# The down matrices of the expert loop issued from ScalarE's queue

## The chip, the cores and the metric

The kernel runs on one core of a Trainium2 chip. The metric is the device time of one launch in microseconds; lower is better. The core has five engines that run their own instruction streams: TensorE (PE), VectorE (DVE), ScalarE (ACT), GpSimd (POOL) and SyncE (SP). They meet through semaphores alone. SP and ACT can each start transfers (DMAs) on a queue of their own; sixteen DMA engines carry them out.

## What is computed

One layer of an encoder for 320 tokens (256 of one request group, 64 of another), all in float32: a mixing sublayer (a projection, attention beside a convolution, gates, an output projection, a layer norm) and then a sublayer of experts. The experts take most of the time:

```python
logits = (x @ w_router + b_router).astype(jnp.float32)
top_val, top_idx = lax.top_k(logits, TOP_K)            # 4 of 32
gate = jax.nn.softmax(top_val, axis=-1)
...
gt = jnp.minimum(xe @ w_gate[e] + b_gate[e], SWIGLU_LIMIT)
up = jnp.clip(xe @ w_up[e] + b_up[e], -SWIGLU_LIMIT, SWIGLU_LIMIT)
h = gt * jax.nn.sigmoid(SWIGLU_ALPHA * gt) * (up + 1.0)
return h @ w_down[e] + b_down[e]
```

Each expert has three matrices of 1024 x 1024 in float32. Each token goes through four experts, and the sum of their outputs, weighted with `gate`, goes into a second layer norm.

## The kernel before

The mixing sublayer and the router fill the first 430 us or so. What follows is the expert loop. The tokens of one expert are taken in groups of 32 slots, so an expert has one group or several, by how many tokens chose it. The router's counts are turned into tables in SBUF: `order` gives the expert at each of 32 places, `tbl[k]` the number of the first group of place k, `tbl[32]` the number of all groups. Experts 0 and 1 always stand at places 0 and 1, since their matrices are loaded ahead; behind them places 3, 6, 9, ... hold the experts with most tokens, in falling order, and the two places between them experts with few.

The weights have six buffers of 4 MB, two for each kind: `WG`, `WU` and `WD`, each with a buffer for even and one for odd places (`par`). Every matrix is loaded in two halves of 2 MB (`load_halves`, L237, which calls `load_half`, L234; the profile puts the DMA instructions of the loop under L235).

For one group PE does, in this order: the gate products (`gate_or_up`, matmuls L1334, biases L1339), the combine of the previous group's first token tile (L1349), the up products, the combine of the second tile, the gather of the next group's tokens (L1322), a small product (L1381), the combine of the third tile (L1351), and the down products (L1390). Gate and up wait for each half of their matrix (L1330), down likewise (L1388). PE raises `gate_half`, `gate_done`, `up_half`, `up_done`, `down_half` and `down_done`, once in each group.

VectorE clamps the gate (L948), waits for ScalarE's sigmoid, multiplies (L950), adds a tile of combined output to the accumulator (L938), does the same for up (L955, L958), transposes (L963), and so on. ScalarE has two steps in a group: the sigmoid (L614, with a table load ahead of it) and the copy of the down result out of PSUM (L616), after `down_done`. GpSimd makes the selection matrices (L454 to L463) and one-hot columns (L468, L469). VectorE, GpSimd and SP read the tables at every expert (`value_load`); ScalarE reads only the total number of groups, once (L610), and then runs one flat loop.

SP feeds the weights (L349 to L355). For each place from 2 on it reads `used`, the number of groups up to and including the place whose buffers are to be taken (two places earlier), and the expert's number `e`. Then it waits for `gate_half`, starts the first half of WG, waits for `gate_done`, starts the second half, and so on through WU and WD: twelve steps in strict order, all on SP's queue. Places 0 and 1 are loaded ahead of the loop. Behind it SP loads the rows of the last layer norm into WG[0] (L357 to L365).

Of the kernel before, what the change touches and what calls it, by code (L numbers as in the profile page):

```python
# [28 lines left out]
E = 32  # L29
# [16 lines left out]
def encoder_step(nc, x_prompt, x_sample, cache_k, cache_v, state_conv, w_in, b_in, rel_bias, w_att_o,  # L46
# [13 lines left out]
    wg_v, wu_v, wd_v = (w[0].rearrange("e (p c) n -> e p c n", p=P) for w in (w_gate, w_up, w_down))  # L60
# [8 lines left out]
    with ctx:  # L69
# [31 lines left out]
        WG, WU, WD = (wbuf[2], wbuf[0]), (wbuf[1], wbuf[5]), (wbuf[4], wbuf[3])  # L101
# [65 lines left out]
        tbl = SB[96:97, M0 + 1504:M0 + 1538].bitcast(I32)  # L167
        order = SB[96:97, M0 + 1538:M0 + 1570].bitcast(I32)
# [55 lines left out]
        def sem(name):  # L224
            if name not in sems:
                sems[name] = ctx.enter_context(nc.semaphore(name))
            return sems[name]
# [6 lines left out]
        def load_half(eng, buf, src, name, h):  # L234
            eng.dma_start(buf[:, 4 * h:4 * h + 4, :], src[:, 4 * h:4 * h + 4, :]).then_inc(sem(f"{name}_{h}"), 16)  # L235

        def load_halves(eng, buf, src, name, used=None, count=None):  # L237

            for h in range(2):
                if used is not None:  # L240
                    eng.wait_ge(sem(used[h]), count)
                load_half(eng, buf, src, name, h)

        def weights(v, e):
            return v[bass.ds(e, 1)].rearrange("a p c n -> p (a c) n")
# [19 lines left out]
        def _(sp):  # L265
# [83 lines left out]
            with sp.Fori(1, E // 2) as q:  # L349
                for par in range(2):  # L350
                    used = sp.value_load(tbl[0:1, bass.ds(q * 2 + (par - 1), 1)], min_val=1, max_val=200)
                    e = sp.value_load(order[0:1, bass.ds(q * 2 + par, 1)], min_val=0, max_val=E - 1)
                    load_halves(sp, WG[par], weights(wg_v, e), f"wg{par}", ["gate_half", "gate_done"], used)
                    load_halves(sp, WU[par], weights(wu_v, e), f"wu{par}", ["up_half", "up_done"], used)
                    load_halves(sp, WD[par], weights(wd_v, e), f"wd{par}", ["down_half", "down_done"], used)  # L355

            used = sp.value_load(tbl[0:1, E - 1:E], min_val=1, max_val=200)  # L357
            sp.wait_ge(sem("gate_done"), used)
# [21 lines left out]
        def _(pool):  # L380
# [34 lines left out]
            for tt, (_, r) in enumerate(TT):  # L415
                link(pool.tensor_scalar(xtok[0:r, tt, :], xtok[0:r, tt, :], ALPHA, None, ALU.mult))
                pool.tensor_tensor(xtok[0:r, tt, :], xtok[0:r, tt, :], bout_bc[0:r], ALU.add).then_inc(sem("xr_ready"), 1)
                pool.wait_ge(sem("xr_ready"), tt + 1)
# [64 lines left out]
        def _(act):  # L483
# [123 lines left out]
            act.copy(rankT, PS[0:E, 5, 0:T]).then_inc(sem("rankT_ready"), 1)  # L607

            act.wait_ge(sem("tables_done"), 1)
            total = act.value_load(tbl[0:1, E:E + 1], min_val=1, max_val=200)  # L610
            with act.Fori(0, total) as i:
                act.wait_ge(sem("gmin"), i + 1)
                act.wait_ge(sem("h_ready"), i + 1)
                act.activation(tin, PS[:, 0, 0:256], ACT.Sigmoid, scale=SW_ALPHA).then_inc(sem("sig"), 1)  # L614
                act.wait_ge(sem("down_done"), i + 1)
                act.copy(ysb, PS[:, 2, 256:512]).then_inc(sem("y_sb"), 1)  # L616

            for tt in range(3):
# [406 lines left out]
        def _(pe):  # L1026
# [270 lines left out]
            for s, (_, r) in enumerate(TT):  # L1297
                ins = pe.matmul(PS[:, 7, 3 * E:4 * E], ones16[0:r], chosen[0:r, s, :], start=(s == 0), stop=(s == 2))
# [135 lines left out]
```

## Time and profile before

| | |
|---|---|
| median of 3 runs | 1406.92 us (1404.81 to 1411.04) |
| the profiled execution | 1409.85 us |
| its span, first to last instruction | 1408.1 us |
| groups in the expert loop | 58, in 32 places |
| mean granted TensorE clock | 0.965 of full |
| PE busy | 1282.1 us (91%), of it L1334 447.1, L1390 221.0 |
| VectorE, ScalarE, GpSimd busy | 615.1, 206.5, 135.1 us |
| moved by DMA | 459.68 MB, 326 GB/s over the span |
| of it on SP's queue (q1), on ACT's (q10) | 459.03 MB, 0.33 MB |
| chain that ended last | PE 64%, DMA 31% (w_down 27%, w_up 4%) |

The page gives busy times, a picture of the span in 40 slices of 35.2 us, and the chain of work that ended last, followed back through whatever released each step. A large DMA share in that chain means that PE stood at the end of a transfer, directly or by way of a buffer. Busy shares are averages over stages that differ, so the argument goes by stretches.

### The profile page before, as it was taken

What the parts mean: (1) busy time and instruction counts of PE and PEld (TensorE: products, weight loads), DVE (VectorE), ACT (ScalarE), POOL (GpSimd) and SP (SyncE); (2) the same over time, 40 slices, a digit from 0 to 9 for tenths busy, and PEclk for the clock granted to TensorE, in tenths of its full rate; (3) what the DMA queues carried; (4) which work ended last, traced back from release to release, by engine and by line L of the source; (5) the groups of instructions that cost most, each with busy time, mean ns of one, the idle gap of its engine ahead of it and who ended that gap; (6) DMA issues with size and microseconds to landing.
All of it is one profiled execution on the core that took longest, in us unless ns stands there. A gap on an engine that the chain in (4) does not pass through costs nothing.

```text
span 1408.1 us, 40782 instructions
## 1 busy us (share of the span) xinstructions
PE 1282.1 (91%) x16754; PEld 732.1 (52%) x16755; DVE 615.1 (44%) x1156; ACT 206.5 (15%) x386; POOL 135.1 (10%) x337
## 2 busy tenths in 40 slices
PE   8999999999989899989989989898897988769994
PEld 6777675576544445545545545454453444335552
DVE  0369993452165334433434334333343333223445
ACT  1111112342011111111111111111010110101111
POOL 3900000000001100010001000100010000001010
PEclk9999999999988999999999999999999999989997
DMA  9333233615959980798998998999999999999996
GB/s 296 114 129 128 85 129 141 224 61 238 340 238 410 428 367 0 296 427 359 429 429 340 430 431 358 429 428 428 429 428 429 429 429 428 429 429 429 428 429 236
DMA packets 57170, 459.68 MB, mean 326 GB/s; under 512 B 5426, under 2 KB 9250, under 8 KB 32539
## 3 DMA queue, kind: packets, MB, share of 16 engines
q1 hardware_dynamic: 56858, 459.03, 79.2%
q10 hardware_dynamic: 289, 0.33, 0.1%
q8 instruction: 16, 0.26, 0.1%
q14 instruction: 7, 0.06, 0.0%
HBM read 455.14 MB, written 4.73 MB: 327 GB/s over the span
## 4 chain that ended last, share of the span: by engine, by line
PE 64%; DMA 31%; DVE 2%; ACT 1%; issue 1%; another core or an unknown queue 0%; SPq 0%; POOLq 0%; POOL 0%; ACTq 0%; DVEq 0%
DMA SB<-in_w_down_dram 27%; PE PS L1334 17%; PE PS L1048 12%; PE PS L1390 10%; PE PS L1322 4%; DMA SB<-in_w_up_dram 4%; PE PS L1349 3%; PE PS L1230 3%; PE PS L1159 2%; PE PS L1114 2%; PE PS L1241 2%; PE PS L1067 1%; PE PS L1074 1%; PE PS L1029 1%; PE PS L1351 1%
## 5 line engine op out<-in xcount | busy, mean ns | idle before, releaser
L1334 PE MATMUL PS<-SB 128*32 128x256 f32 x7424 | 447.1, 393 | 65.3 <-DMA SB<-in_w_up_dram 35.2
L1334 PEld LDWEIGHTS PS<-SB 128*32 128x32 f32 x7424 | 240.3, 113 | 255.4 <-issue 72.8
L1390 PE MATMUL PS<-SB 128*32 128x256 f32 x3712 | 221.0, 388 | 24.4 <-DMA SB<-in_w_down_dram 23.9
L938 DVE SCALAR_TENSOR_TENSOR SB<-PS,SB 128x1024 f32<-128x1024 f32 x176 | 193.7, 1100 | 8.9 <-PE PS L1349 4.0
L948 DVE TENSOR_SCALAR PS<-PS 128x256 f32<-128x256 f32 x58 | 25.1, 432 | 387.1 <-PE PS L1339 387.1
L1390 PEld LDWEIGHTS PS<-SB 128*32 128x32 f32 x3712 | 115.7, 112 | 111.7 <-DMA SB<-in_w_down_dram 31.6
L1048 PE MATMUL PS<-SB 128*128 128x320 f32 x640 | 172.7, 433 | 0.0
L1048 PEld LDWEIGHTS PS<-SB 128*128 128x128 f32 x640 | 121.4, 190 | 50.4
L677 DVE SCALAR_TENSOR_TENSOR SB<-SB 128x350 f32<-128x350 f32 x240 | 118.6, 583 | 0.0
L616 ACT COPY SB<-PS 128x256 f32<-128x256 f32 x58 | 21.6, 372 | 661.2 <-PE PS L1390 661.2
L1322 PE MATMUL PS<-SB 128*32 128x256 f32 (+1 forms) x1416 | 97.7, 390 | 0.0
L955 DVE TENSOR_SCALAR PS<-PS 128x256 f32<-128x256 f32 x58 | 25.1, 432 | 155.6 <-PE PS L1339 155.6
L1349 PE MATMUL PS<-SB 32*128 32x256 f32 x944 | 85.0, 430 | 0.6 <-ACT SB L616 0.6
L468 POOL CAST SB<-SB 96x1 bf16 x58 | 10.6, 183 | 729.1 <-PE PS L1381 728.9
L614 ACT ACT_TABLE_LOAD x58 | 74.4, 1283 | 6.0 <-DVE SB L909 5.0
L1322 PEld LDWEIGHTS PS<-SB 128*32 128x32 f32 (+1 forms) x1416 | 34.0, 108 | 55.1 <-issue 45.2
L1349 PEld LDWEIGHTS PS<-SB 32*128 32x128 f32 x944 | 37.5, 186 | 39.2 <-issue 39.2
L614 ACT ACTIVATE SB<-PS 128x256 f32<-128x256 f32 x58 | 22.2, 384 | 179.4 <-DVE PS L948 179.4
L500 ACT ACTIVATE SB<-PS,SB 128x320 f32 x40 | 21.1, 527 | 141.1 <-PE PS L1048 141.1
L1159 PE MATMUL PS<-SB 128*128 128x320 f32 x128 | 37.9, 439 | 0.0
L1230 PE MATMUL PS<-SB 128*128 128x320 f32 x128 | 36.2, 447 | 0.5 <-ACT SB L565 0.5
L950 DVE TENSOR_TENSOR SB<-SB,PS 128x256 f32<-128x256 f32 x58 | 24.4, 421 | 26.1 <-ACT SB L614 26.1
(220 smaller groups left out, 893.3 us busy)
## 6 DMA issues: line engine op xcount, KB each, us to landing
SB<-in_w_gate_dram SPq DMA_DIRECT2D x64, 2048.0 KB, 30.3
SB<-in_w_up_dram SPq DMA_DIRECT2D x64, 2048.0 KB, 35.9
SB<-in_w_down_dram SPq DMA_DIRECT2D x64, 2048.0 KB, 39.1
SB<-in_w_in_dram SPq DMA_DIRECT2D x13, 2048.0 KB, 7.9
SB<-in_w_pw_dram SPq DMA_DIRECT2D x2, 2048.0 KB, 9.9
SB<-in_w_att_o_dram SPq DMA_DIRECT2D x2, 2048.0 KB, 7.9
SB<-in_w_out_dram SPq DMA_DIRECT2D x2, 2048.0 KB, 9.9
SB<-in_w_in_dram SPq DMA_DIRECT2D x4, 512.0 KB, 9.5
```

The lines of the kernel that those rows point to most:

```text
L614: act.activation(tin, PS[:, 0, 0:256], ACT.Sigmoid, scale=SW_ALPHA).then_inc(sem("sig"), 1)
L677: dve.scalar_tensor_tensor(yc[:, c, :], uext[:, c, bass.ds(k, CONVN)], dwT[:, c, bass.ds(k, 1)], yc[:, c, :], ALU.mult, ALU.add).then_inc( ...
L938: dve.scalar_tensor_tensor(y, ps, gcol[:, tt:tt + 1], y, ALU.mult, ALU.add).then_inc(sem("yadd"), 1)
L1048: ins = pe.matmul(PS[:, t, 0:T], ring[s][:, c, P * t:P * t + P], xT[:, c, :], start=(c == 0), stop=(c == KC - 1))
L1114: ins = pe.matmul(PS[:, 2 * s + tt, :], xT[:, c, t0:t0 + r], ring[s][:, c, :], start=(c == 0), stop=(c == KC - 1))
L1159: ins = pe.matmul(PS[:, 6 + j % 2, 0:T], ring[s][:, c, P * t:P * t + P], zc[:, c, :], start=(c == 0), stop=(c == KC - 1))
L1230: ins = pe.matmul(PS[:, t % 4, 0:T], ring[s][:, c, P * (t % 4):P * (t % 4) + P], oT[:, c, :], start=(c == 0), stop=(c == KC - 1))
L1241: ins = pe.matmul(PS[:, 2 * tt + s, :], mixT[:, c, P * tt:P * tt + P], ring[s][:, c, :], start=(c == 0), stop=(c == KC - 1))
L1322: ins = pe.matmul(PS[32 * q:32 * q + 32, 3, 0:256], sel[r, tt, :], x_part(tt, q // 2)[:, k], start=(tt == 0), stop=(tt == 2))
L1334: ins = pe.matmul(PS[32 * q:32 * q + 32, bank, 0:256], xg[:, c, :], buf[:, c, 256 * q:256 * q + 256], start=(c == 0), stop=False)
L1349: ins = pe.matmul(PS[:, bank + q, 0:256], scat[r, P * tt:P * tt + P], ysb[r, :], start=True, stop=True)
L1390: ins = pe.matmul(PS[32 * n:32 * n + 32, 2, 256:512], hT[:, ck, :], WD[par][:, ck, 256 * n:256 * n + 256], start=(ck == 0), stop=(ck == KC ...
```

## The change

SP's loop loses its third line: it loads WG and WU only. ScalarE's flat loop over all groups becomes a loop over the places from 2 to 31, in pairs. For each it reads three table entries, the first and the last group of the place two earlier and the number of the expert to be loaded, runs the groups of that earlier place, and then starts both halves of WD on its own queue, with no wait on a semaphore: the copy of the last group has already waited for its `down_done`. The groups of the last two places follow in a loop of their own. The loads of places 0 and 1 stay on SP.

```diff
@@ block.sync
                     load_halves(sp, WG[par], weights(wg_v, e), f"wg{par}", ["gate_half", "gate_done"], used)
                     load_halves(sp, WU[par], weights(wu_v, e), f"wu{par}", ["up_half", "up_done"], used)
-                    load_halves(sp, WD[par], weights(wd_v, e), f"wd{par}", ["down_half", "down_done"], used)
@@ block.scalar
             act.wait_ge(sem("tables_done"), 1)
-            total = act.value_load(tbl[0:1, E:E + 1], min_val=1, max_val=200)
-            with act.Fori(0, total) as i:
+            def group(i):
+
                 act.wait_ge(sem("gmin"), i + 1)
                 act.wait_ge(sem("h_ready"), i + 1)
                 act.activation(tin, PS[:, 0, 0:256], ACT.Sigmoid, scale=SW_ALPHA).then_inc(sem("sig"), 1)
                 act.wait_ge(sem("down_done"), i + 1)
                 act.copy(ysb, PS[:, 2, 256:512]).then_inc(sem("y_sb"), 1)
+
+            with act.Fori(1, E // 2) as k:
+                for par in range(2):
+                    first = act.value_load(tbl[0:1, bass.ds(k * 2 + (par - 2), 1)], min_val=0, max_val=200)
+                    last = act.value_load(tbl[0:1, bass.ds(k * 2 + (par - 1), 1)], min_val=1, max_val=200)
+                    e = act.value_load(order[0:1, bass.ds(k * 2 + par, 1)], min_val=0, max_val=E - 1)
+                    with act.Fori(first, last) as i:
+                        group(i)
+                    load_halves(act, WD[par], weights(wd_v, e), f"wd{par}")
+            rest = act.value_load(tbl[0:1, E - 2:E - 1], min_val=0, max_val=200)
+            total = act.value_load(tbl[0:1, E:E + 1], min_val=1, max_val=200)
+            with act.Fori(rest, total) as i:
+                group(i)
```

## Rows read from the trace of the kernel before

**Rows 1.** The page's 40 slices of 35.2 us: GB/s moved.

```profile
GB/s 296 114 129 128 85 129 141 224 61 238 340 238 410 428 367 0 296 427 359 429 429 340 430 431 358 429 428 428 429 428 429 429 429 428 429 429 429 428 429 236
```

**Rows 2.** Stretches: from:to, length, busy of each engine, PEclk, DMA share, GB/s.

```profile
524.00:572.00 48.00, 48.00 (x873) 26.38 (x867) 20.54 (x37) 7.26 (x11) 6.06 (x20) 1.00 0.00 0
...
662.00:667.00 5.00, 5.00 (x99) 2.99 (x92) 0.72 (x2) 1.66 (x2) 1.15 (x3) 1.00 0.03 13
...
851.00:855.00 4.00, 4.00 (x80) 2.42 (x76) 0.63 (x2) 1.41 (x2) 1.15 (x3) 1.00 0.02 8
...
935.00:1200.00 265.00, 231.02 (x3875) 120.12 (x3871) 94.06 (x165) 30.58 (x45) 22.74 (x75) 0.95 1.01 429
```

**Rows 3.** Timeline of SP's queue: start, us until both are issued, what.

```profile
572.70 2.14 SPq L235 DMA_DIRECT2D SB<-in_w_gate_dram  x2
...
666.54 2.14 SPq L235 DMA_DIRECT2D SB<-in_w_gate_dram  x2
...
855.43 2.14 SPq L235 DMA_DIRECT2D SB<-in_w_gate_dram  x2
...
978.47 12.08 SPq L235 DMA_DIRECT2D SB<-in_w_down_dram  x2
...
1112.52 2.14 SPq L235 DMA_DIRECT2D SB<-in_w_gate_dram  x2
```

**Rows 4.** w_down's issues: size and median us to landing; then ns of one issue.

```profile
SB<-in_w_down_dram SPq DMA_DIRECT2D x64, 2048.0 KB, 39.1
...
L235 SPq DMA_DIRECT2D SB<-in_w_down_dram x64: 328/333/7799, 372.7 to 1344.1; - x64
```

**Rows 5.** ScalarE's timeline: copies that end groups, start and us (58 in all).

```profile
585.19 0.37 ACT L616 COPY SB<-PS 128x256 f32<-128x256 f32 x1 [9.97 <-PE PS L1390]
600.25 0.37 ACT L616 COPY SB<-PS 128x256 f32<-128x256 f32 x1 [9.97 <-PE PS L1390]
614.60 0.37 ACT L616 COPY SB<-PS 128x256 f32<-128x256 f32 x1 [9.96 <-PE PS L1390]
...
635.97 0.37 ACT L616 COPY SB<-PS 128x256 f32<-128x256 f32 x1 [16.33 <-PE PS L1390]
...
1388.52 0.37 ACT L616 COPY SB<-PS 128x256 f32<-128x256 f32 x1 [10.62 <-PE PS L1390]
```

**Rows 6.** PE's timeline in the first group of place 6: its waits.

```profile
624.17 3.09 PE L1334 MATMUL PS<-SB 128*32 128x256 f32 x32 [2.87 <-DMA SB<-in_w_up_dram]
...
633.97 1.93 PE L1390 MATMUL PS<-SB 128*32 128x256 f32 x32 [1.41 <-DMA SB<-in_w_down_dram]
```

**Rows 7.** Timeline of 1328:1345, all engines: one change of expert.

```profile
1328.53 0.35 POOL L454 TENSOR_TENSOR SB<-SB 128x96 f32<-128x96 f32 x1 [2.70 <-issue]
...
1330.16 1.28 ACT L614 ACT_TABLE_LOAD   x1
...
1333.78 0.38 ACT L614 ACTIVATE SB<-PS 128x256 f32<-128x256 f32 x1 [2.33 <-DVE PS L948]
1333.84 3.18 PEld L1334 LDWEIGHTS PS<-SB 128*32 128x32 f32 x64 [0.33 <-issue]
...
1334.53 1.28 DVE L938 SCALAR_TENSOR_TENSOR SB<-PS,SB 128x1024 f32<-128x1024 f32 x1
...
1337.55 0.71 PE L1349 MATMUL PS<-SB 32*128 32x256 f32 x8
...
1344.13 0.37 ACT L616 COPY SB<-PS 128x256 f32<-128x256 f32 x1 [9.96 <-PE PS L1390]
```

**Rows 8.** DMA issues of 3.5:4.3 us: size, median us to landing.

```profile
SB<-in_w_in_dram SPq DMA_DIRECT2D x2, 512.0 KB, 10.4
SB<-in_state_conv_dram ACTq DMA_DIRECT2D x1, 120.0 KB, 7.8
```

**Rows 9.** DMA queues in 8:9.5 us: packets, MB, share of the 16 engines.

```profile
q1 hardware_dynamic: 154, 0.29, 79.6%
q10 hardware_dynamic: 42, 0.11, 29.0%
```

## The prediction

> **What bounds the kernel now.** I read the slices of the page first: in most of the expert loop they stand at 427 to 431 GB/s, but one is at 0 (528 to 563 us) and a few later ones at 340 to 359 [rows 1]. The table of stretches shows what PE does meanwhile [rows 2]: from 935 to 1200 us 429 GB/s are moved without a pause and PE is busy for 231 of 265 us, near its limit too; in 524:572 nothing is moved while PE is 100% busy, and the same holds in three short holes of 5 us, of which the first and the last stand there (662:667 and 851:855). Each such hole is time in which all six weight buffers are full and an expert with many groups is being computed.
>
> The SP rows show why it ends [rows 3]. At 572.70 the gate half of the last group of the expert at place 3 frees WG, and the first load after the hole starts; 666.54 is the same for place 6. Between them lie three experts' loads. One matrix is two halves of 2048 KB [rows 4], 4.19 MB, or 9.8 us at 429 GB/s; an expert takes 29.35 us and three of them 88.05 us. The ACT copies end the groups [rows 5]: 58 of them, the last at 1388.52, 14.35 us apart where nothing waits (600.25 to 614.60) and 15.06 at every second change of expert (585.19 to 600.25). Counted between the SP issues, places 0, 1, 2 have one group each, place 3 has 7, places 6, 9, 12 have 4, places 15, 18, 21 have 3, places 24, 27 to 30 have 2, all others 1.
>
> A check that the model of one queue, served in order, is right. With t = 0 at 572.70, the queue holds G5 U5 D5 G6 U6 D6 in this order (G, U, D for gate, up, down; the number is the place). U6 should land after five matrices, 48.9 us, plus a lag; PE resumes on it at 624.17, t = 51.5: the lag is 2.6. D6 should land at 58.7 + 2.6 = 61.3; PE resumes on it at 633.97, t = 61.3 [rows 6]. After D's second half PE needs only 32 matmuls, 1.93 us, to close the group. That is the best order there is: the last thing to land is the last thing used.
>
> **The change part by part.** Removed: SP's two waits and two issues for D. They free nothing on SP: the wait behind them is the gate half of the next group, later in PE's own order than this group's down. What moved from SP past those waits therefore starts no earlier.
>
> Added on ScalarE, once per expert: two issues, three value loads, a loop boundary. One issue takes 0.33 us where it isn't held [rows 4], 0.67 for two. The same three loads and boundary cost GpSimd 2.70 us of "issue" at the most [rows 7]. ACT's table load started right behind the copy, at 1330.16; with 3.4 us put in between and its own 1.28 it ends at 1334.8. The sigmoid started at 1333.78, so it is 1.0 us late; VectorE's sum behind it (L938, 1334.53 and 1.28 long) then ends at 1336.8, and the combine on PE that wants it starts at 1337.55 [rows 7]. Cost nothing, with 0.7 us of cover; each microsecond beyond it would cost up to 30, one for each place. If an issue is held on ACT as SP's are (two took 12.08 us [rows 3]), the group behind it is late; bound 0 to 5 us for each large expert, taken 0.
>
> D is issued at the group's end, 1.4 to 3 us later than now, but 20 us of G and U are in flight: nothing.
>
> What costs is the order of arrival. D is now on a queue of its own and no longer waits behind G and U. Do two queues share? At the start of the kernel both are in use. state_conv, issued on ACT at 3.9 us, landed 7.8 us later, while SP's pieces of w_in issued in the same stretch, earlier or later, took 10.4 [rows 8]; in 8:9.5 SP's backlog moved 0.29 MB and ACT's few rows 0.11 MB [rows 9]. So ACT's transfers pass the backlog. Their packets are unlike SP's, so 0.11 to 0.29 is only a bound of the share; for equal packets on both sides I take one half. The Trainium skill (DMA: Bandwidth & Descriptors, "Queues, rings and completion order") says that each DMA engine goes round robin over its queue rows, packet by packet; the rows just named agree as far as they go, and by that rule too the share of equal packets is a half.
>
> Cycle from t = 0 at 572.70, all in microseconds of full rate (a matrix is 9.8). G5 alone until 9.8; U5 has 3.1 at 12.9, when D5 is issued (end of a group, 585.19, plus copy). From there half rate each: U5 done at 26.3. D6 is issued at 27.9 (600.25 + 0.4, less 572.70) and stands behind D5, which is done at 32.5; G6 has 3.1 then and is done at 45.9. D6 is done at 52.1, U6 has 3.1; D7, issued at 42.3 (614.60 + 0.4), goes on sharing, so U6 needs 13.4 more: 65.5, lands at 68.1. D7 is then two thirds loaded, for nothing: its expert comes last. PE resumes on U6's second half at 68.1 instead of 51.5. Behind that half lie the rest of the up, bias, combines, gather and the whole down: in an undisturbed group 1335.67 (half of the up at 1333.84) to the copy at 1344.13, 8.4 us [rows 7]. The group ends at 76.5 instead of 63.3 (635.97): **13.2 us late**. Two corrections of opposite sign: TensorE's granted clock falls to its 1.2 GHz level after waits like 2.87 us, and the 32 matmuls behind one took 3.09 instead of 1.93 [rows 6], +1.2 to 1.7 for each cycle; if the queues alternate by whole halves, U6 lands at 63.7 + 2.6, -1.8. They cancel and I leave both out.
>
> The next T is 76.5 + 1.9 (half a gate) + 14.35 for each group beyond the second. Four groups: 107.1 instead of 93.9 (measured 666.54 - 572.70 = 93.84). Above 88.05 all of it is DMA hole, so the whole 13.2 is lost.
> - Places 3, 6, 9, 12: 4 x 13.2 = 52.8.
> - Places 15, 18, 21 (three groups): 92.8 each, 278.4 in all, a hole of 4.7 in each; before 855.43 to 1112.52 = 257.1. Lost 21.3, of which 9 had been backlog that the next part would have had to wait out.
> - Places 24 to 31: before 1112.52 to 1388.5 = 276.0. After: 78.4 to the last group of place 24 (not DMA bound). From there U25, three matrices of 26, three of 27 and D28, which slips ahead of U27, are 78.3 of transfer: U27 lands at 81, its group ends at 89.4, and then 8 more groups of PE, 116.6, bound the end: 206.0. Together 284.4, lost 8.4.
> Sum 52.8 + 21.3 + 8.4 = 82.5. The profiled execution took 1409.85, so 1492.3; it lies 2.9 above the median of the runs, so **1489**.
>
> **The rivals.** *Unequal shares.* With D at two fifths, U6 lands at 59.3 + 2.6 and D6 just in time: the cycle is late by 4.4 only, the sum is about 25, 1432. With D at 0.28 (0.11 of 0.40 MB [rows 9]) D5 lands at 50.5, after place 5 wants it at 38, D6 only at 81, and the cycle is late by 20: the sum is about 135, 1540. Equal packets speak against both.
>
> *Order kept.* If the 16 DMA engines served both queues by age, or D's issue came too late to pass anything, arrival would be as before and the time 1407 to 1412. The early landing of state_conv [rows 8] speaks against it.
>
> *Faster.* Two queues could move more than one. Place: the 880 us of transfer of the loop (30 x 29.35); price: 8.8 us for each per cent. No stretch of the rows moves over 429 GB/s. Against the 82 us of order it decides only from 9%; with the order kept, from 0.8%. A better order than now can't be had, since up to a large expert's first group the same six matrices must land. The Trainium skill (the same page, "Specifications") gives a ceiling of 435 GB/s for a core's port to SBUF; by it the gain ends at 1.5%, some 13 us, 1394 with the order kept.
>
> *ACT held at the issue.* If both queues have one limit on what is outstanding, ACT stands for up to 8 us and the sigmoid of the next group comes after its cover: up to 5 us for each of nine large experts, 45 on top, 1534.
>
> **How the numbers follow.** Half shares, sum 60 to 110: 0.60. Weaker effect by uneven shares, 15 to 60: 0.13. Stronger, by shares or a held ACT, over 110: 0.12. Order kept: 0.10. Faster: 0.05. The range goes to 1430 at the low end (two fifths) and to 1540 at the high end (0.28), leaving out the two last cases and the tails. A measurement of this kernel tells about 0.5%, 7 us, from no change: faster 0.05, same 0.09, slower 0.86.
>
> **What would show it.** In the profile after: a queue of ACT with about 126 MB beside SP's 333; PE's waits on w_up and w_gate grow to over 10 us in each cycle and those on w_down are nearly gone; DMA holes near 62 us once, 18 us three times, some 5 us three times; the median from issue to landing of w_down falls from 39.1 to 20 to 25 us; issues of WG 107 us apart where they were 94. Groups inside an expert stay 14.35 us apart; if they don't, ScalarE's additions aren't covered. The forecast is wrong if w_down still takes about 39 us to land (no sharing), or if PE still waits on w_down in the large experts (shares below a half).

## The result and the profile after

| | before | after |
|---|---|---|
| median of the runs | 1406.61 us (4 runs) | 1497.38 us (4 runs, 1495.29 to 1498.59) |
| ratio, with its 95% interval | | 1.0636 (1.0617 to 1.0655) |
| the profiled execution, its span | 1409.85, 1408.1 us | 1498.59, 1496.9 us |
| mean granted TensorE clock | 0.965 | 0.930 |

The change makes the kernel 6.4% slower; the forecast was 1489. The page of the changed kernel, first the slices (now 37.4 us each), then the queues, the end of the chain, and the landing times:

```profile
GB/s 282 123 113 112 113 112 189 127 85 355 237 425 427 424 4 117 430 428 202 430 412 211 430 368 271 428 359 432 429 372 427 357 432 428 428 428 428 428 426 57
...
q1 hardware_dynamic: 48218, 333.20, 54.8%
q10 hardware_dynamic: 8929, 126.17, 19.8%
...
DMA SB<-in_w_up_dram 25%; PE PS L1346 21%; PE PS L1060 12%; PE PS L1402 10%; PE PS L1334 4%; PE PS L1361 4%; DMA SB<-in_w_gate_dram 3%; PE PS L1242 2%; PE PS L1171 2%; PE PS L1126 2%; PE PS L1253 2%; PE PS L1079 1%; PE PS L1086 1%; PE PS L1363 1%
...
SB<-in_w_up_dram SPq DMA_DIRECT2D x64, 2048.0 KB, 38.2
SB<-in_w_down_dram ACTq DMA_DIRECT2D x60, 2048.0 KB, 23.5
```

Lines have moved: L1334, L1390 and L1349 of before are L1346, L1402 and L1361 here, the sigmoid and the copy of ScalarE L613 and L615. Three things are to be seen against [rows 1, 4]. w_down lands 23.5 us after its issue, not 39.1. In the chain w_up has taken w_down's place. And the rate, where it is full, is what it was (427 to 432 GB/s), but more slices fall below it.

The holes in stretches of their own (columns as in [rows 2]):

```profile
525.00:587.00 62.00, 62.00 (x1120) 33.94 (x1116) 25.96 (x46) 3.39 (x9) 7.23 (x23) 1.00 0.00 0
676.00:694.00 18.00, 18.00 (x333) 9.98 (x327) 7.03 (x13) 2.95 (x5) 2.65 (x8) 1.00 0.03 15
892.00:910.00 18.00, 18.00 (x332) 9.97 (x328) 6.74 (x13) 3.30 (x5) 2.31 (x7) 1.00 0.04 17
1000.00:1004.00 4.00, 4.00 (x82) 2.37 (x77) 0.58 (x2) 0.37 (x1) 1.15 (x3) 1.00 0.01 4
```

The hole at place 3 has grown from 48 to 62 us, those at places 6 and 12 from 5 and 4 to 18, and at place 15, where before there was none, stand 4. The first loads of each cycle on SP's queue, which answer to [rows 3]:

```profile
587.05 2.14 SPq L235 DMA_DIRECT2D SB<-in_w_gate_dram  x2
...
694.94 2.14 SPq L235 DMA_DIRECT2D SB<-in_w_gate_dram  x2
...
910.58 2.14 SPq L235 DMA_DIRECT2D SB<-in_w_gate_dram  x2
...
1191.68 2.14 SPq L235 DMA_DIRECT2D SB<-in_w_gate_dram  x2
```

587.05 is 14.35 us after the 572.70 of before, and from 587.05 to 694.94 it is 107.9 us, where it was 93.8. PE in the first group of place 6 in between, against [rows 6], with the copy on ScalarE that ends the group:

```profile
634.25 3.57 PE L1346 MATMUL PS<-SB 128*32 128x256 f32 x32 [2.99 <-DMA SB<-in_w_gate_dram]
...
644.05 3.64 PE L1346 MATMUL PS<-SB 128*32 128x256 f32 x32 [5.48 <-DMA SB<-in_w_up_dram]
653.76 3.64 PE L1346 MATMUL PS<-SB 128*32 128x256 f32 x32 [6.07 <-DMA SB<-in_w_up_dram]
...
664.37 0.37 ACT L615 COPY SB<-PS 128x256 f32<-128x256 f32 x1 [25.54 <-PE PS L1402]
```

U6's second half is there at 653.76, t = 66.7 counted from 587.05; before it was 51.5. The down products, which waited last before, wait for nothing; the group ends at t = 77.3 instead of 63.3. Last the queues from 615 to 655 us:

```profile
DMA packets 1175, 17.15 MB, mean 429 GB/s; under 512 B 128, under 2 KB 128, under 8 KB 128
...
q1 hardware_dynamic: 589, 8.60, 50.5%
q10 hardware_dynamic: 586, 8.55, 50.3%
```

429 GB/s in all, half of it for D: here the same bytes come at the same rate, in another order. The experiments ask whether that is the whole of the loss.

### The profile page after: what moved, and what is told of

It is laid out like the page before. It is cut to its first block, busy times and chain, and to the rows that moved or that the text cites. A ratio compares the mean times of both kernels' runs of the same rounds, so it can differ in the third digit from the quotient of the medians.

```text
span 1496.9 us, 41221 instructions
## 1 busy us (share of the span) xinstructions
PE 1297.9 (87%) x16754; PEld 738.3 (49%) x16755; DVE 612.4 (41%) x1156; ACT 164.2 (11%) x354; POOL 135.0 (9%) x337
## 4 chain that ended last, share of the span: by engine, by line
PE 67%; DMA 28%; DVE 2%; ACT 1%; another core or an unknown queue 1%; issue 1%; POOLq 0%; SPq 0%; POOL 0%; ACTq 0%; DVEq 0%
DMA SB<-in_w_up_dram 25%; PE PS L1346 21%; PE PS L1060 12%; PE PS L1402 10%; PE PS L1334 4%; PE PS L1361 4%; DMA SB<-in_w_gate_dram 3%; PE PS L1242 2%; PE PS L1171 2%; PE PS L1126 2%; PE PS L1253 2%; PE PS L1079 1%; PE PS L1086 1%; PE PS L1363 1%
## 5 line engine op out<-in xcount | busy, mean ns | idle before, releaser
L1346 PE MATMUL PS<-SB 128*32 128x256 f32 x7424 | 466.5, 405 | 161.9 <-DMA SB<-in_w_up_dram 122.5
L1346 PEld LDWEIGHTS PS<-SB 128*32 128x32 f32 x7424 | 245.3, 116 | 363.3 <-issue 161.7
L1402 PE MATMUL PS<-SB 128*32 128x256 f32 x3712 | 212.3, 381 | 0.0
L960 DVE TENSOR_SCALAR PS<-PS 128x256 f32<-128x256 f32 x58 | 25.1, 433 | 360.7 <-PE PS L1351 360.7
L1402 PEld LDWEIGHTS PS<-SB 128*32 128x32 f32 x3712 | 114.7, 110 | 79.7 <-DVE SB L975 9.1
L967 DVE TENSOR_SCALAR PS<-PS 128x256 f32<-128x256 f32 x58 | 25.1, 433 | 265.5 <-PE PS L1351 265.5
L615 ACT COPY SB<-PS 128x256 f32<-128x256 f32 x58 | 21.6, 372 | 739.8 <-PE PS L1402 739.8
L1334 PE MATMUL PS<-SB 128*32 128x256 f32 (+1 forms) x1416 | 99.0, 394 | 0.0
L1361 PE MATMUL PS<-SB 32*128 32x256 f32 x944 | 87.9, 443 | 0.6 <-ACT SB L615 0.6
L467 POOL CAST SB<-SB 96x1 bf16 x58 | 10.6, 183 | 816.9 <-PE PS L1393 816.7
L1334 PEld LDWEIGHTS PS<-SB 128*32 128x32 f32 (+1 forms) x1416 | 34.4, 110 | 56.7 <-issue 47.1
L1361 PEld LDWEIGHTS PS<-SB 32*128 32x128 f32 x944 | 38.6, 191 | 41.7 <-issue 41.7
L613 ACT ACTIVATE SB<-PS 128x256 f32<-128x256 f32 x58 | 22.2, 383 | 184.8 <-DVE PS L960 184.7
## 6 DMA issues: line engine op xcount, KB each, us to landing
SB<-in_w_down_dram ACTq DMA_DIRECT2D x60, 2048.0 KB, 23.5
```

The costliest lines, as they stand in the source:

```text
L1334: ins = pe.matmul(PS[32 * q:32 * q + 32, 3, 0:256], sel[r, tt, :], x_part(tt, q // 2)[:, k], start=(tt == 0), stop=(tt == 2))
L1346: ins = pe.matmul(PS[32 * q:32 * q + 32, bank, 0:256], xg[:, c, :], buf[:, c, 256 * q:256 * q + 256], start=(c == 0), stop=False)
L1361: ins = pe.matmul(PS[:, bank + q, 0:256], scat[r, P * tt:P * tt + P], ysb[r, :], start=True, stop=True)
L1402: ins = pe.matmul(PS[32 * n:32 * n + 32, 2, 256:512], hT[:, ck, :], WD[par][:, ck, 256 * n:256 * n + 256], start=(ck == 0), stop=(ck == KC ...
```

## The experiments

The theory: two queues share the DMA engines half and half; D so gets ahead of the U that is wanted first (6.7 us in a cycle), the last thing to land is a U, behind which lies more of a group (6.5 us), and each such delay adds to a hole. The rivals: ScalarE's added work or the later issue costs; or a second stream as such does. Where a loss is split by parts below, it is counted from profile to profile: the four cycles of places 3, 6, 9 and 12 (before: from the first load at 433.08 to the one at 855.43), the three of places 15, 18 and 21 (to 1112.52), and the end, up to the last copy (1388.52).

### All but the issues on the second queue (e1_one_queue_late)

ScalarE keeps the loop over places, with two of its three table reads; SP issues D, both halves only after the copy of the last group.

```diff
+                    sp.wait_ge(sem("y_sb"), used + 1)
+                    load_halves(sp, WD[par], weights(wd_v, e), f"wd{par}")
...
-                    e = act.value_load(order[0:1, bass.ds(k * 2 + par, 1)], min_val=0, max_val=E - 1)
...
-                    load_halves(act, WD[par], weights(wd_v, e), f"wd{par}")
```

> ScalarE runs the loop over places as in the changed kernel (but for one table entry), and D is issued by SP again, both halves only after the copy that ends the last group: same programs on ACT and the same late issue, but one queue. Theory (the cost is the order in which two queues deliver): D stays behind G and U, U6 lands about 51.5 us after the first load, holes 49 and three of 5 us; 1404 to 1412. Rival (the cost is ScalarE's added work or the later issue): 1450 to 1500, most of the 90 us stay.

Measured: 1407.96 us, ratio to before 1.0002 (0.9990 to 1.0014). Its profile:

```profile
SB<-in_w_down_dram SPq DMA_DIRECT2D x64, 2048.0 KB, 37.0
...
523.00:570.00 47.00, 47.00 (x851) 25.74 (x847) 19.81 (x36) 2.64 (x7) 5.69 (x18) 1.00 0.00 0
```

The hole at place 3 is the old one. Two of the added table reads and the loop boundaries cost nothing that can be measured, and neither does the later issue. The third read and the two issues are not in this kernel on ScalarE; in the changed one the issues take 0.85 us for both halves, and the groups inside an expert stay 14.35 us apart. So the loss comes with the move of D to the second queue.

### One queue, U behind D (e2_up_last)

```diff
                     load_halves(sp, WG[par], weights(wg_v, e), f"wg{par}", ["gate_half", "gate_done"], used)
-                    load_halves(sp, WU[par], weights(wu_v, e), f"wu{par}", ["up_half", "up_done"], used)
                     load_halves(sp, WD[par], weights(wd_v, e), f"wd{par}", ["down_half", "down_done"], used)
+                    load_halves(sp, WU[par], weights(wu_v, e), f"wu{par}", ["up_half", "up_done"], used)
```

> The kernel before with one edit: SP's order is G, D, U instead of G, U, D, all on one queue. Nothing is shared, but U lands last. Theory: in the cycle from place 3 to 6, U6 lands at 62.4, the group ends at 72.8 with 2 us for the clock, 9.5 late; four such cycles 38, three of 89.1 against 257.1 another 10, the rest 1: 1456. Rival (two streams on the DMA engines disturb each other, the order is harmless): 1407.

Measured: 1452.65 us, ratio 1.0318 (1.0287 to 1.0350). SP's first loads of two cycles, and PE's waits between them:

```profile
582.11 2.14 SPq L235 DMA_DIRECT2D SB<-in_w_gate_dram  x2
...
683.38 2.14 SPq L235 DMA_DIRECT2D SB<-in_w_gate_dram  x2
```

```profile
639.46 3.24 PE L1334 MATMUL PS<-SB 128*32 128x256 f32 x32 [10.67 <-DMA SB<-in_w_up_dram]
644.26 1.93 PE L1334 MATMUL PS<-SB 128*32 128x256 f32 x32 [1.56 <-DMA SB<-in_w_up_dram]
```

U6 is there at t = 62.15 (expected 62.4), the cycle is 101.3 long instead of 93.8. Nothing shares anything here, and half of the changed kernel's loss is back: the order alone costs. By parts, the four cycles lost 31.3 us (expected 38), the next three 8.6 (10), the end 3.8 (1). In the four cycles the 2 us for the clock were often not due: behind the last wait for U the 32 matmuls took 1.93 us in two of them (here after 1.56 us of waiting) and 3.64 in the other two.

### U on ScalarE's queue instead of D (e3_up_on_act)

```diff
-                    load_halves(sp, WU[par], weights(wu_v, e), f"wu{par}", ["up_half", "up_done"], used)
+                    load_halves(sp, WD[par], weights(wd_v, e), f"wd{par}", ["down_half", "down_done"], used)
...
-                    load_halves(act, WD[par], weights(wd_v, e), f"wd{par}")
+                    load_halves(act, WU[par], weights(wu_v, e), f"wu{par}")
```

> The changed kernel with U and D exchanged: ACT issues U after the last group's copy, SP issues G and D. The queues share as before, but D, the last matrix a group uses, now lands last. Theory: D6 lands at about 70, the group ends 9 us late instead of 14 (the 6.5 us between the ends of up and down are saved, a wait of its own for U5 and the clock cost 1 to 2); 36 for four cycles, 9 for the next three, about -5 at the end: 1447. Rival (what costs is a second queue as such, whichever matrix is on it): 1497 as the changed kernel.

Measured: 1463.6 us, ratio 1.0379 (1.0346 to 1.0412), 34 us below the changed kernel.

```profile
581.98 2.14 SPq L235 DMA_DIRECT2D SB<-in_w_gate_dram  x2
...
685.62 2.14 SPq L235 DMA_DIRECT2D SB<-in_w_gate_dram  x2
```

```profile
650.76 3.64 PE L1402 MATMUL PS<-SB 128*32 128x256 f32 x32 [4.38 <-DMA SB<-in_w_down_dram]
```

The cycle takes 103.6, late by 9.8 (expected 9), with D6 at t = 68.8. So which matrix lands last counts, not only that there are two queues. The sum was 17 us too low all the same, and not in these cycles: the four lost 35.2 us (expected 36), but the next three 15.0 (9), and the end lost 3.9 where a gain of 5 was expected. In the cycles of three groups the rate is 413 GB/s over two stretches of 100 us (1060 to 1260). Part of this is short holes ahead of the first loads at 1071.26 and 1163.18: 253 GB/s in 1068:1071.5 and 229 in 1160:1163.5. What makes up the rest there, and the 9 us at the end, stays open.

### Rows of 4 KB for D, for all, for G and U (e4, e5, e6)

The halves are cut into four transfers of 512 KB, for the matrices named; PE waits for 64 instead of 16 on their semaphores. The cut for D alone:

```diff
+            if name[:2] in ('wd',):
+                for c in range(4 * h, 4 * h + 4):
+                    eng.dma_start(buf[:, c, :], src[:, c, :]).then_inc(sem(f"{name}_{h}"), 16)
...
-                                pe.wait_ge(sem(f"wd{par}_{ck // 4}"), q * 16 + 16)
+                                pe.wait_ge(sem(f"wd{par}_{ck // 4}"), q * 64 + 64)
```

> The changed kernel with each half of D as four transfers of 512 KB, so that a row of a partition is 4 KB instead of 16 KB; G and U as they are. Tells how two backlogs are shared. By packets, one for one: D gets about a fifth, 0.85 MB in 10 us beside 3.4; D5 lands near 64, after place 5 wants it, D6 near 81, the group ends 20 late: about 1550, and PE waits for w_down. By bytes or time: halves as before, 1497.

> The changed kernel with all halves of G, U and D as four transfers of 512 KB. Control for e4: rows are alike on both queues again, so by either rule the halves are equal: 1490 to 1505, unless rows of 4 KB move slower than the 428 GB/s.

> The changed kernel with the halves of G and U as four transfers of 512 KB, D as it is. By packets D gets four fifths: D5 and D6 land soon, U6 at about 71 instead of 66.7, the group ends some 4 us later than in the changed kernel: about 1535. By bytes or time: 1497.

Measured: D alone 1604.52 us, ratio 1.1386 (1.1323 to 1.1449); all 1535.02, 1.0893 (1.0840 to 1.0946); G and U 1540.54, 1.0932 (1.0881 to 1.0983). The queues (packets, MB, share of the engines), first with D in pieces, 625 to 665 us, then with all in pieces, 615 to 655:

```profile
q1 hardware_dynamic: 940, 13.57, 79.7%
q10 hardware_dynamic: 945, 3.41, 21.2%
```

```profile
DMA packets 4499, 16.39 MB, mean 410 GB/s; under 512 B 499, under 2 KB 499, under 8 KB 4499
...
q1 hardware_dynamic: 2249, 8.22, 51.8%
q10 hardware_dynamic: 2250, 8.17, 51.0%
```

The time with D as a whole and G and U in pieces, 1540.54, is near the 1535 expected of sharing by packets and far from the 1497 of sharing by bytes, though some of the difference to 1497 may be the slower rows of 4 KB. The control with all in pieces was meant to give the time of the changed kernel and gave 38 us more. Two things can have done this. Rows of 4 KB move at 410 GB/s and not at 428: for the loop's 377 MB that is 39 us, if all of it were on the path. And ScalarE is busy longer with its issues: eight take 3.83 us where two took 0.85, and 9.53 where they are held, the sigmoid comes later, and PE's combine waits for VectorE for 25.1 us in all, which it does not in the changed kernel. How the 38 us divide isn't shown.

D in pieces is slower than the 1550 expected, for a reason that belongs to a rival. ScalarE's timeline there, then what the chain that ended last is made of:

```profile
617.05 3.90 ACTq L237 DMA_DIRECT2D SB<-in_w_down_dram  x8
...
633.62 32.07 ACTq L237 DMA_DIRECT2D SB<-in_w_down_dram  x8
667.70 0.38 ACT L617 ACTIVATE SB<-PS 128x256 f32<-128x256 f32 x1 [33.97 <-issue]
...
PE 61%; ACTq 25%; DVE 4%; issue 4%; ACT 3%; SPq 2%; DMA 1%; POOLq 0%; POOL 0%; DVEq 0%
```

The second set of eight issues holds ScalarE for 32 us, and the sigmoid behind it comes 34 us after the last activity. Three of the eight pass in 1.37 us, 17 us behind the first set; the other five go one at a time, 5.4 to 7.5 us apart. The expectation had the cause wrong: PE was to wait for w_down, and in the whole profile it never does. At the combine it waits 283.6 us in all for VectorE, which waits for the sigmoid, and the chain that ended last is 25% issues of ScalarE and 1% DMA. So this run shows the shares by its packets, but its time is that of a held ScalarE and says nothing on what a share of a fifth costs.

### D at two fifths, and at a third (e7, e8)

D in three transfers of 3, 3 and 2 chunks, or in four of 2 chunks, each with a semaphore of its own (rows of 12, 12 and 8 KB, or of 8 KB). The first:

```diff
+            if name[:2] == "wd":
+                for k, c in enumerate((slice(0, 3), slice(3, 6), slice(6, 8))):
+                    eng.dma_start(buf[:, c, :], src[:, c, :]).then_inc(sem(f"{name}_{k}"), 16)
+                return
...
-                            if ck % 4 == 0:
-                                pe.wait_ge(sem(f"wd{par}_{ck // 4}"), q * 16 + 16)
+                            if ck % 3 == 0:
+                                pe.wait_ge(sem(f"wd{par}_{ck // 3}"), q * 16 + 16)
```

> The changed kernel with D in three transfers of 3, 3 and 2 chunks: rows of 12, 12 and 8 KB beside the 16 KB of G and U, so by packets D gets 10.67 of 26.67, two fifths (170 beside 256 GB/s). The sharing arithmetic then says: D5 done at 37.3 and D6 at 61.7, both just in time; U6 lands at 56.7 + 2.6 = 59.3 (not the 61.9 of the rival's text, its sum of 4.4 had been made with 59.3), the group ends at 67.7, 69.5 with the clock, 6 us late instead of 14. 24 for four cycles, about 3 for the next three, which are bound by DMA then, 10 at the end: 1444. If D's share made no difference: 1497.

> The same with D in four transfers of 2 chunks, rows of 8 KB: by packets D gets a third (142 beside 284 GB/s). Now D is the late one: D5 done at 42.2, place 5 waits for it, D6 done at 71.5, the group ends at about 76, 12.7 us late, and PE waits on w_down where in the changed kernel it waits on w_up. About 1485: slower again than two fifths. If a smaller share were simply better (nearer to the old order): under 1444.

Measured: two fifths 1450.15 us, ratio 1.0294 (1.0259 to 1.0330); a third 1506.17, 1.0696 (1.0661 to 1.0731). The queues from 620 to 660 us and the largest wait of PE in all (us, times, longest), first at two fifths, then at a third:

```profile
q1 hardware_dynamic: 698, 10.14, 59.7%
q10 hardware_dynamic: 688, 7.00, 41.4%
...
PE PS L1350 <- DMA SB<-in_w_up_dram: 90.0, 21, 5.9
```

```profile
q1 hardware_dynamic: 775, 11.37, 66.9%
q10 hardware_dynamic: 774, 5.69, 34.0%
...
PE PS L1407 <- DMA SB<-in_w_down_dram: 155.7, 31, 6.3
```

With D's share going down from a half by two fifths to a third the time goes 1497, 1450, 1506: better and then worse, and at the turn PE's waits change from w_up to w_down. ScalarE isn't held in either kernel (no issue takes over 390 ns). A story about ScalarE or about two streams as such has no turn there; the arithmetic of arrival had it at the right place. It was 6 us low for two fifths (the cycle from place 3 to 6 is 100.4 us, late by 6.5, expected 6) and 21 low for a third, where the cycle is 110.2 against 106.6 by the expected end of the group (76 + 1.9 + 28.7). No share that was tried comes near 1407: the order of one queue was the best of them.

## Why the prediction was right, point by point

**What bounds the kernel.** The model of full buffers and holes held. PE needs D last, and U last costs 46 us on one queue. That the old order can't be bettered stays an argument: eight kernels with other orders, issues or packet sizes were run, and none is faster than the one before (the nearest, at 1407.96, has its order).

**ScalarE's additions at nothing.** Right, and with less added than I had counted: in the changed kernel the sigmoid's table is loaded 25 times instead of 58, so in many groups after an issue there is no load of 1.28 us. Where there is one it ends at 604.41 and the sigmoid starts at 604.43, about 0.2 us later than 0.47 us behind VectorE's clamp (603.79), which is its distance where no load is in the way (618.14 to 618.61); 1.0 us late was forecast, and both lie inside the cover. ScalarE was never held at an issue in the changed kernel (each took 339 to 390 ns); the rival of the held ScalarE is real, but needs more transfers outstanding, as with D in pieces.

**Half shares.** 8.60 beside 8.55 MB. The rows at the start of the kernel [rows 8, 9] had shown sharing, and a fraction only as a bound. The 0.28 in bytes did not come from the sizes of the packets: ScalarE's queue moved 42 with more bytes to each against SP's 154, too few to be taken for a backlog.

**The cycle.** Late by 13.2 was forecast, 14.0 measured:

| from the first load of the cycle | before | forecast | after |
|---|---|---|---|
| PE resumes on U6's second half | 51.5 | 68.1 | 66.7 |
| rest of the group behind it | | 8.4 | 10.6 |
| the group ends | 63.3 | 76.5 | 77.3 |
| next first load, four groups | 93.8 | 107.1 | 107.9 |
| the same, three groups | 79.5 to 89.5 | 92.8 | 93.2 to 94.1 |

I had left out two corrections as equal. The one for whole halves gives 66.3, near the measured 66.7, but by luck: the queues do not alternate by whole halves (65 and 64 packets in 635:640, and 16 and 10 in 636:637). What the sum lacked is D's own lag. D5 is issued at 599.82, but ScalarE's queue moves only 0.44 MB from 600 to 605, which is 2 us at half the rate, so its first bytes move at about 603, t = 15.9; the sum had them at 12.9, or 14.5 with G5's lag of 1.6 us. By the sum's own working each microsecond that D starts later brings U6 one earlier: 68.1 less 1.4 is 66.7. The correction for the clock was mis-sized: I had +1.2 to 1.7 from a wait of 2.87 us; after 6.07 us of waiting the granted clock is 0.50 of full in 653.5:657, the 1.2 GHz level, and stays low beyond the 32 matmuls (3.64), which makes the biases 0.44 instead of 0.29 and the combine 0.96 instead of 0.71 as well, so that it came to 2.2. The 14.0 are thus 13.2 less 1.4 plus 2.2: that 13.2 came so close is in part these two errors cancelling.

**The sum.** The first loads stand at 433.54, 587.05, 694.94, 803.37 and 910.58 against 433.08, 572.70, 666.54, 761.70 and 855.43: +54.7 for places 3 to 12 (forecast 52.8), and 0.5 that was there at the start. From there to 1191.68, three cycles, 281.1 against 257.1: +24.0 (21.3). From there to the last copy at 1477.34, 285.7 against 276.0: +9.7 (8.4). Together they are the difference of the spans (88.8), against 82.5. The missing 6.3 us are about 1.9, 2.7 and 1.3 in these three parts and the 0.5 at the start. In the cycle followed above 0.8 are missing, the clock's 2.2 less the 1.4 of D's lag; the others I have not taken apart.

**The rivals.** Unequal shares: none between equal packets. The rival's price was right in its direction: two fifths costs 43 us, and not 25; the text's landing of U6 there, 59.3 + 2.6, should have read 59.3 in all, and the term for the clock was left out. Its price for 0.28 (135 us) was not tested. Order kept: wrong, as w_down's 23.5 us to landing shows. Faster by two streams: the fullest slice of the changed kernel moves 432 GB/s, that of the kernel before 431. ScalarE held: not in the changed kernel, as said. The signs named beforehand came, among them that PE no longer waits for w_down.

## What to carry to other kernels

A queue served in order is also a schedule: if transfers are the bound and each buffer is filled in the order in which it is used, moving one stream to a second queue gives that stream a share of the engines whether its data is wanted soon or not. Before such a move work out what will be the last thing to land and how much work lies behind it. If two queues must be used, the packet sizes set the shares; but more and smaller transfers take longer to issue, and can hold the engine that issues them.

## What the runs showed of the hardware that I had not expected

- With both queues backlogged the shares of bytes follow the packet sizes closely: 50:50 with 16 KB on both sides, 41:59 with 12, 12 and 8 KB against 16, 33:67 with 8 against 16, 20:80 with 4 against 16, and 78:22 with 16 against 4.
- The number of transfers outstanding on ScalarE's queue has a limit: of eight of 512 KB, issued 17 us behind another eight of which 1.23 MB (two transfers and a part) had been moved, three passed and five held the engine, for 32.07 us in all, in which it computes nothing. With transfers of 2 MB, at most four or so outstanding, each issue took 0.34 to 0.39 us.
- Rows of 16 KB move at 429 GB/s, with two queues as with one; rows of 4 KB at 410 with two queues and at 408 with one (640:645 with G and U in pieces).
